# Mixing weights kept split across two passes, and the last norm's sums and spread set inside the first feed-forward blocks

## The chip, the cores and the metric

The program runs on one core of one Trainium2 chip. The metric is the device time of one launch in microseconds; a run is one execution, and the time given for a kernel is the median of its runs. TensorE (PE), VectorE (DVE), ScalarE (ACT), GpSimd (POOL) and SyncE (SP, which only issues transfers here) each execute their own instructions in order, and semaphores order them against each other.

## The reference

Two layers of a block on 1024 tokens and, in the first layer, 256 context tokens (1280 columns in layer 0, 1024 in layer 1), with 1024 features. All of it is computed in f32. What matters here is the end of each layer:

```
y = concatenate([retention, window attention, gated delta]) @ w_out[layer]
x = x + g1 * y
x = x + g2 * swiglu(rmsnorm(x, norm_ffn_w[layer]) * (1.0 + sc2) + sh2, w_ffn_in[layer], w_ffn_out[layer])
```

w_out is 1024 x 1024. swiglu is silu(h @ w1) * (h @ w3) @ w2 with 2816 inner features. The context tokens go through the same in layer 0 with their own scales. Everything ahead of the mixed outputs is left as it is by the change.

## The kernel before

Features lie on partitions (8 chunks of 128, index m for output and k for input), tokens along the free dimension. The tokens are cut into slices (`token_slices`): 256, 512 and 512 columns in layer 0, 512 and 512 in layer 1. The last slice is the "late" one, the others are "early". `mixed_ffn` (L1025) is one stage per layer: the mixing with w_out, the norm behind it, and the feed-forward loops.

A product of f32 precision takes three matmuls (`three_passes`, L927): the weight is split into a rounded part (hi) and the rest (lo), and so is the moving operand. A weight chunk of 128 x 1024 comes by one 512 KB transfer into `raw[u]`, ACT rounds it into `w_hi[u]` (`round`, L917), DVE subtracts and writes `w_lo[u]` (`rest`, L922); u alternates between two buffers, and one split is enough for one output chunk m.

The mixing has 16 passes (`passes`, L1061). Passes 0 to 7 take the early slices, m = 0 to 7, and passes 8 to 15 take the late slice, again m = 0 to 7. So each of the 8 weight chunks is loaded, rounded and split twice. In a pass PE does 8 k times 3 matmuls per slice into `bank[m % 2][slice]` (`pe_mix`, L1071); DVE then adds the product into x (`dve_add`, L1088, line L1095 in rows), ACT squares the new x (`square`, L359) and DVE adds the square to `total` (`gather`, L367). The list of each engine is written out by hand (`act_mix` L1098, `dve_mix` L1115): in pass i ACT squares and then rounds the weight of pass i+2, and DVE adds, gathers and then splits it.

The norm (`TurnedNorm`, L937) comes in two groups, early and late. Once `total` of a group is complete: PE sums over features (`pe_sums`, L965), ACT takes the root (L978), DVE inverts (L990) and lays it on diagonals (`dve_lay`, L995), PE spreads it over the partitions (`pe_spread`, L973). Then each slice takes 8 steps: DVE scales a chunk (L1006, into the two buffers of `ffn_prod`), ACT adds the shift and rounds (`act_round`, L985), DVE forms the rest (L1014). The results go into the tiles `ys` and `yr` (o_ys_hi, yr_lo and so on in rows), which held the mixer's outputs. The early group's sums and spread stand inside passes 8 and 9 (behind k = 4), and its steps are dealt out over passes 9 to 15 (`spots`, L1064), on DVE one of a pass's steps ahead of the gather and the weight split and the others behind them.

The feed-forward begins with `pe_first` (L1136), which does the first two output units u = 0 and 1. Before, it does u = 0 of the early slices, the late group's sums, u = 1 of the early slices, the late spread, and then both units of the late slice; each k of u = 0 waits for its norm step. Loops over the other units follow (`pe_up`, `pe_down`), in which `a_hi` and `a_lo` hold the gated products. These two tiles (128 x 5120 each) are idle until then. SP issues the weight transfers (L1263, L1267) as a buffer's split is done; POOL issues the eight loads of x (L1275) once the first two weight chunks have landed.

## Time and profile before

| | us |
|---|---|
| median of 3 runs | 3723.64 |
| lowest and highest run | 3721.9, 3729.55 |
| the profiled execution | 3734.98 |
| its span, first to last instruction | 3733.2 |
| PE busy | 3327.0 (89%) |
| DVE busy | 1644.3 (44%) |
| ACT busy | 1060.6 (28%) |
| mean granted TensorE clock | 0.931 |

The busy time of PE counts from a matmul's start to its modelled end, so successive matmuls overlap in it, and a matmul at the lower clock counts as longer busy. The distance from one start to the next tells more. Times of rows count from the start of the span. The stage `mixed_ffn` of layer 0 starts its matmuls at 977 us, that of layer 1 at 2884 us.

### The profile page before, as it was taken

What the parts mean: (1) busy time and instruction counts of PE and PEld (TensorE: products, weight loads), DVE (VectorE), ACT (ScalarE), POOL (GpSimd) and SP (SyncE); (2) the same over time, 40 slices, a digit from 0 to 9 for tenths busy, and PEclk for the clock granted to TensorE, in tenths of its full rate; (3) what the DMA queues carried; (4) which work ended last, traced back from release to release, by engine and by line L of the source; (5) the groups of instructions that cost most, each with busy time, mean ns of one, the idle gap of its engine ahead of it and who ended that gap; (6) DMA issues with size and microseconds to landing.
All of it is one profiled execution on the core that took longest, in us unless ns stands there. A gap on an engine that the chain in (4) does not pass through costs nothing. (4 is left out here: it accounts for less than half of the span.)

```text
span 3733.2 us, 56373 instructions
## 1 busy us (share of the span) xinstructions
PE 3327.0 (89%) x21762; PEld 2792.9 (75%) x21762; DVE 1644.3 (44%) x2735; ACT 1060.6 (28%) x1934; POOL 667.8 (18%) x762
## 2 busy tenths in 40 slices
PE   4989856977899999999999999757887999999998
PEld 2878745866778888888887788646775778888886
DVE  5365776632453322223136465775633532322234
ACT  3344134612232121121213244134512331122112
POOL 1232763222000000000001132762222000000000
PEclk7999967988999999999999999868997999999998
DMA  4456185086521111111112465285194311111111
GB/s 175 150 190 202 62 282 157 18 233 183 196 64 40 35 39 40 39 39 34 39 40 83 139 194 189 74 281 149 38 263 168 110 42 51 47 49 51 45 51 62
DMA packets 245240, 405.31 MB, mean 109 GB/s; under 512 B 76083, under 2 KB 146483, under 8 KB 244662
## 3 DMA queue, kind: packets, MB, share of 16 engines
q1 hardware_dynamic: 239222, 382.76, 32.9%
q0 software_dynamic: 5824, 19.93, 1.4%
q8 instruction: 126, 2.06, 0.2%
q14 instruction: 68, 0.56, 0.0%
HBM read 289.97 MB, written 100.56 MB: 105 GB/s over the span
## 5 line engine op out<-in xcount | busy, mean ns | idle before, releaser
L924 DVE TENSOR_TENSOR ffn_w_lo<-ffn_raw,ffn_w_hi 128x1024 fp32r<-128x1024 f32 x164 | 200.8, 1225 | 500.6 <-ACT ffn_w_hi L920 495.4
L849 PE MATMUL frt_acc<-frt_w_hi,frt_h_hi 128*128 128x472 f32 x928 | 364.7, 393 | 51.2 <-DVE frt_w_lo L728 26.5
L930 PE MATMUL ffn_bank<-yr_hi,ffn_w_hi 128*128 128x512 f32 (+1 forms) x1040 | 386.3, 371 | 24.9 <-DVE ffn_w_lo L924 22.0
L930 PE MATMUL ffn_bank<-o_ys_hi,ffn_w_hi 128*128 128x512 f32 (+1 forms) x1040 | 387.2, 372 | 7.1 <-DVE o_ys_lo L1014 6.1
L933 PE MATMUL ffn_bank<-o_ys_lo,ffn_w_hi 128*128 128x512 f32 (+1 forms) x1040 | 384.7, 370 | 0.0
L934 PE MATMUL ffn_bank<-o_ys_hi,ffn_w_lo 128*128 128x512 f32 (+1 forms) x1040 | 384.1, 369 | 0.0
L933 PE MATMUL ffn_bank<-yr_lo,ffn_w_hi 128*128 128x512 f32 (+1 forms) x1040 | 384.0, 369 | 0.0
L934 PE MATMUL ffn_bank<-yr_hi,ffn_w_lo 128*128 128x512 f32 (+1 forms) x1040 | 383.9, 369 | 0.0
L849 PE MATMUL frt_acc<-frt_w_hi,frt_h_lo 128*128 128x472 f32 x928 | 355.8, 383 | 0.0
L849 PE MATMUL frt_acc<-frt_w_lo,frt_h_hi 128*128 128x472 f32 x928 | 355.1, 383 | 0.0
L930 PE MATMUL ffn_bank<-ffn_a_hi,ffn_w_hi 128*128 128x512 f32 (+1 forms) x880 | 324.3, 368 | 0.8 <-DVE ffn_a_lo L1191 0.8
L933 PE MATMUL ffn_bank<-ffn_a_lo,ffn_w_hi 128*128 128x512 f32 (+1 forms) x880 | 324.3, 368 | 0.0
L934 PE MATMUL ffn_bank<-ffn_a_hi,ffn_w_lo 128*128 128x512 f32 (+1 forms) x880 | 323.7, 368 | 0.0
L920 ACT ACTIVATE ffn_w_hi<-ffn_raw 128x1024 fp32r<-128x1024 f32 x164 | 172.4, 1051 | 450.8 <-PE ffn_bank L930 443.1
L1234 DVE SCALAR_TENSOR_TENSOR x<-ffn_bank,mod,x 128x512 f32 (+3 forms) x240 | 166.7, 696 | 280.1 <-PE ffn_bank L934 279.3
L849 PEld LDWEIGHTS frt_acc<-frt_w_hi,frt_h_hi 128*128 128x128 f32 x928 | 179.0, 193 | 88.1 <-issue 26.4
L930 PEld LDWEIGHTS ffn_bank<-yr_hi,ffn_w_hi 128*128 128x128 f32 x1040 | 196.8, 189 | 64.1 <-DVE ffn_w_lo L924 25.3
L930 PEld LDWEIGHTS ffn_bank<-o_ys_hi,ffn_w_hi 128*128 128x128 f32 x1040 | 197.4, 190 | 45.2 <-issue 7.0
L1198 DVE TENSOR_TENSOR ffn_prod<-total,ffn_bank 128x512 f32<-128x512 f32 (+1 forms) x110 | 69.7, 634 | 360.9 <-PE ffn_bank L934 264.3
L934 PEld LDWEIGHTS ffn_bank<-o_ys_hi,ffn_w_lo 128*128 128x128 f32 x1040 | 197.0, 189 | 33.3
L933 PEld LDWEIGHTS ffn_bank<-o_ys_lo,ffn_w_hi 128*128 128x128 f32 x1040 | 197.6, 190 | 32.4 <-issue 0.5
L934 PEld LDWEIGHTS ffn_bank<-yr_hi,ffn_w_lo 128*128 128x128 f32 x1040 | 197.0, 189 | 32.9
(359 smaller groups left out, 5785.9 us busy)
## 6 DMA issues: line engine op xcount, KB each, us to landing
ffn_raw<-w_ffn SPq DMA_DIRECT2D x132, 512.0 KB, 3.6
x<-ada_w SPq DMA_DIRECT2D x15, 2048.0 KB, 9.2
proj<-frt_out SPq DMA_DIRECT2D x116, 236.0 KB, 2.0
x<-proj SPq DMA_DIRECT2D x60, 384.0 KB, 4.6
frt_raw<-w_in SPq DMA_DIRECT2D x96, 236.0 KB, 4.3
ffn_raw<-w_out SPq DMA_DIRECT2D x32, 512.0 KB, 3.7
met_pr<-proj SPq DMA_DIRECT2D x20, 768.0 KB, 6.5
met_vn<-pack SPq DMA_DIRECT2D x20, 640.0 KB, 6.3
```

The costliest lines, as they stand in the source:

```text
L849: mm = pe.matmul(acc[q % NA][:, 0:GW], a[:, k, tok], b[:, k, :], start=(k == 0 and i == 0), stop=(k == KC - 1 and i == 2))
L920: act.activation(self.hi[u][:], self.raw[u][:], ACT.Copy).then_inc(self.rounded[u], 1)
L924: dve.tensor_tensor(self.lo[u][:], self.raw[u][:], self.hi[u][:].bitcast(F32), ALU.subtract).then_inc(self.ready[u], 1)
L930: mm = pe.matmul(out, w_hi, b_hi, start=first, stop=False)
L933: pe.matmul(out, w_hi, b_lo, start=False, stop=False)
L934: return pe.matmul(out, w_lo, b_hi, start=False, stop=last)
L1198: dve.tensor_tensor(prod[:, t0:t0 + ln], sil[:, t0:t0 + ln], bank[1][s][:, 0:ln], ALU.mult).then_inc(free[1][s], 1)
L1234: dve.scalar_tensor_tensor(xs, bank[i][s][:, 0:ln], mod[:, bass.ds(m + 5 * KC, 1), v], xs, ALU.mult, ALU.add).then_inc(free[i][s], 1)
```

## The change

In both layers, after the change:

- There are nine weight splits instead of sixteen (`splits`: chunks 0 to 7, and chunk 5 once more). Chunks 0 to 4 are split into `a_hi` and `a_lo`, which have room for five, and stay there for both passes over the tokens. Chunks 5, 6, 7 and the second 5 use `w_hi` and `w_lo`.
- Passes 8 to 15 take m = 7, 6, 0, 1, 2, 3, 4, 5, so that the two chunks that are still in `w_hi` and `w_lo` come first.
- In passes 0 to 5 the split for two passes later stands ahead of the pass's squares (ACT) and ahead of its adds (DVE). The eighth split waits until PE has begun pass 6. The ninth stands in pass 10, the first feed-forward chunk's split in pass 12 and the second's behind pass 15.
- In passes 9 to 15 ACT takes the pass's first norm step ahead of the square, and DVE takes all steps of a pass ahead of the gather.
- The late group's sums stand inside `pe_first`, behind k = 4 of the last early slice of u = 0, and the late spread stands right behind that slice, ahead of u = 1 of the early slices.

```
...
-    def __init__(self, st, x, total, scratch, slices, name=""):
-        self.x, self.total, self.scratch, self.slices = x, total, scratch, slices
+    def __init__(self, st, x, total, scratch, slices, name="", order=range(KC)):
+        self.x, self.total, self.scratch, self.slices, self.order = x, total, scratch, slices, order
...
     def square(self, act, m, s):
...
         to = self.total[:, t0:t0 + n] if m == 0 else self.scratch[j % 2][:, 0:n]
-        act.activation(to, self.x[:, m, t0:t0 + n], ACT.Square).then_inc(self.squared, 1)
+        act.activation(to, self.x[:, self.order[m], t0:t0 + n], ACT.Square).then_inc(self.squared, 1)
...
         t0, n = self.slices[s]
...
         self.used = [st.sem(f"w_used{u}") for u in range(2)]
-    def round(self, act, u, n):
+    def round(self, act, u, n, first=False):
         act.wait_ge(self.landed[u], n * 16 + 16)
-        act.wait_ge(self.used[u], n + u)
+        if not first:
+            act.wait_ge(self.used[u], n + u)
...
     def rest(self, dve, u, n):
...
     early_s, late_s = list(range(NS - 1)), [NS - 1]
-    MU, MB = KC, KC // 2
+    MU, MB = 1, KC // 2
...
     h = [[ys[half][:, k] if k < 4 else yr[half][:, k - 4] for k in range(KC)] for half in range(2)]
...
-        sq_mix = [Squares(st, x, total, spare, [slices[s] for s in early_s], "early_"), Squares(st, x, total, spare, [slices[s] for s in late_s], "late_")]
+        second = [7, 6, 0, 1, 2, 3, 4, 5]
+        sq_mix = [Squares(st, x, total, spare, [slices[s] for s in early_s], "early_"), Squares(st, x, total, spare, [slices[s] for s in late_s], "late_", second)]
...
         full = [[st.sem(f"full{i}{s}") for s in range(NS)] for i in range(2)]
...
         weights_first = st.sem("weights_first")
-        passes = [(i, i % MU, i // MU) for i in range(2 * MU)]
+        kept = a_hi[:].rearrange("p j n -> p (j n)"), a_lo[:].rearrange("p j n -> p (j n)")
+        KEEP = 5
+        splits = [0, 1, 2, 3, 4, 5, 6, 7, 5]
+        m_landed = [st.sem(f"m_landed{r}") for r in range(2)]
+        m_rounded, m_ready, m_begun = st.sem("m_rounded"), st.sem("m_ready"), st.sem("m_begun")
+        stored = lambda n: [kept[i][:, n * DM:(n + 1) * DM] if n < KEEP else (w.hi, w.lo)[i][1 if n in (6, 8) else 0][:] for i in range(2)]
+        passes = [(i, m, 0) for i, m in enumerate(range(KC))] + [(KC + i, m, 1) for i, m in enumerate(second)]
+        split_of = list(range(KC)) + [7, 6, 0, 1, 2, 3, 4, 8]
         group = [early_s, late_s]
-        gathers = [(MU - 1) * len(g) for g in group]
+        gathers = [(KC - 1) * len(g) for g in group]
         spots = [2, 3, 3, 2, 2, 2, 2] if NS == 3 else [1, 1, 1, 1, 1, 1, 2]
-        def early_steps(m):
-            done = sum(spots[:max(m - 1, 0)])
-            return list(norm.steps(0))[done:done + (spots[m - 1] if m else 0)]
+        def early_steps(q):
+            done = sum(spots[:max(q - 1, 0)])
+            return list(norm.steps(0))[done:done + (spots[q - 1] if q else 0)]
         def pe_mix(pe, i, m, g):
-            n, u = divmod(i, 2)
-            pe.wait_ge(w.ready[u], n + 1)
+            q = i % KC
+            u = q % 2
+            n = split_of[i]
+            if n < 7:
+                pe.wait_ge(m_ready, n + 1)
+            else:
+                pe.wait_ge(w.ready[n - 7], 1)
+            hi, lo_w = stored(n)
...
                 t0, ln = slices[s]
-                if m >= 2:
-                    pe.wait_ge(free[u][s], m // 2)
+                if q >= 2:
+                    pe.wait_ge(free[u][s], q // 2)
...
                     f = slice(k * P, (k + 1) * P)
-                    mm = three_passes(pe, bank[u][s][:, 0:ln], w.hi[u][:, f], w.lo[u][:, f], mixed_in(0, k)[:, t0:t0 + ln], mixed_in(1, k)[:, t0:t0 + ln],
-                                      k == 0, k == KC - 1, w.used[1 - u] if s == group[g][0] and k == 0 else None)
-                    if g == 1 and k == 4 and m == 0:
+                    mm = three_passes(pe, bank[u][s][:, 0:ln], hi[:, f], lo_w[:, f], mixed_in(0, k)[:, t0:t0 + ln], mixed_in(1, k)[:, t0:t0 + ln],
+                                      k == 0, k == KC - 1, {KC: w.used[1], KC + 1: w.used[0]}.get(i) if s == group[g][0] and k == 0 else None)
+                    if s == group[g][0] and k == 0:
+                        mm.then_inc(m_begun, 1)
+                    if g == 1 and k == 4 and q == 0:
                         norm.pe_sums(pe, 0, sq_mix[0].gathered, gathers[0])
-                    if g == 1 and k == 4 and m == 1:
+                    if g == 1 and k == 4 and q == 1:
...
                 mm.then_inc(full[u][s], 1)
-        def dve_add(dve, m, g):
-            u = m % 2
+        def dve_add(dve, i, m, g):
+            q = i % KC
+            u = q % 2
...
                 v = 1 if t0 < CTX else 0
-                dve.wait_ge(full[u][s], m // 2 + 1)
+                dve.wait_ge(full[u][s], q // 2 + 1)
...
                                          ALU.mult, ALU.add).then_inc(free[u][s], 1)
+        def act_split(act, n):
+            if n < 7:
+                act.wait_ge(m_landed[n % 2], n // 2 * 16 + 16)
+                act.activation(stored(n)[0], w.raw[1 - n % 2][:], ACT.Copy).then_inc(m_rounded, 1)
+            elif n == 7:
+                act.wait_ge(m_begun, 7)
+                w.round(act, 0, 0, True)
+            else:
+                act.wait_ge(m_begun, KC + 3)
+                w.round(act, 1, 0, True)
+        def dve_split(dve, n):
+            if n < 7:
+                hi, lo_w = stored(n)
+                dve.wait_ge(m_rounded, n + 1)
+                dve.tensor_tensor(lo_w, w.raw[1 - n % 2][:], hi.bitcast(F32), ALU.subtract).then_inc(m_ready, 1)
+            else:
+                w.rest(dve, n - 7, 0)
+        def splits_beside(i):
+            if i < 6:
+                return [i + 2]
+            return {KC + 2: [8]}.get(i, [])
         def act_mix(act):
-            for u in range(2):
-                w.round(act, u, 0)
+            for n in range(2):
+                act_split(act, n)
             for i, m, g in passes:
+                q = i % KC
+                steps = early_steps(q) if g == 1 else []
+                if g == 0:
+                    for n in splits_beside(i):
+                        act_split(act, n)
+                for step in steps[:1]:
+                    norm.act_round(act, step)
                 for j, s in enumerate(group[g]):
-                    act.wait_ge(free[m % 2][s], m // 2 + 1)
-                    sq_mix[g].square(act, m, j)
-                w.round(act, i % 2, i // 2 + 1)
+                    act.wait_ge(free[q % 2][s], q // 2 + 1)
+                    sq_mix[g].square(act, q, j)
+                if g == 1 and q == 0:
+                    norm.act_root(act, 0)
+                for step in steps[1:]:
+                    norm.act_round(act, step)
                 if g == 1:
-                    if m == 0:
-                        norm.act_root(act, 0)
-                    for step in early_steps(m):
-                        norm.act_round(act, step)
+                    for n in splits_beside(i):
+                        act_split(act, n)
+                if i == KC + 4:
+                    w.round(act, 0, 1)
+            w.round(act, 1, 1)
...
         def dve_mix(dve):
-            for u in range(2):
-                w.rest(dve, u, 0)
+            for n in range(2):
+                dve_split(dve, n)
             for i, m, g in passes:
-                steps = early_steps(m) if g == 1 else []
-                dve_add(dve, m, g)
-                if steps:
-                    norm.dve_step(dve, 0, steps[0])
+                q = i % KC
+                steps = early_steps(q) if g == 1 else []
+                if g == 0:
+                    for n in splits_beside(i):
+                        dve_split(dve, n)
+                dve_add(dve, i, m, g)
+                for step in steps:
+                    norm.dve_step(dve, 0, step)
                 for j in range(len(group[g])):
-                    sq_mix[g].gather(dve, m, j)
-                w.rest(dve, i % 2, i // 2 + 1)
-                if g == 1 and m == 0:
+                    sq_mix[g].gather(dve, q, j)
+                if g == 1 and q == 0:
                     norm.dve_lay(dve, 0)
-                for step in steps[1:]:
-                    norm.dve_step(dve, 0, step)
+                if g == 1:
+                    for n in splits_beside(i):
+                        dve_split(dve, n)
+                if i == KC + 4:
+                    w.rest(dve, 0, 1)
+            w.rest(dve, 1, 1)
...
                 norm.dve_step(dve, 1, step)
...
         def pe_first(pe):
-            def unit(u, s):
+            def unit(u, s, summing=False):
...
                     pe.wait_ge(w.ready[u], MU + 1)
...
                                       h[0][k][:, t0:t0 + ln], h[1][k][:, t0:t0 + ln], k == 0, k == KC - 1, begun)
+                    if summing and k == 4:
+                        norm.pe_sums(pe, 1, sq_mix[1].gathered, gathers[1])
...
             for s in early_s:
-                unit(0, s)
-            norm.pe_sums(pe, 1, sq_mix[1].gathered, gathers[1])
+                unit(0, s, s == early_s[-1])
+            norm.pe_spread(pe, 1, free[1], MB)
...
                 unit(1, s)
-            norm.pe_spread(pe, 1, free[1], MB)
...
                 unit(1, s)
...
             def _(sp):
-                for i, m, g in passes:
-                    if i >= 2:
-                        sp.wait_ge(w.ready[i % 2], i // 2)
-                    sp.dma_start(w.raw[i % 2][:], w_out[m]).then_inc(w.landed[i % 2], 16)
+                for n, m in enumerate(splits):
+                    if n >= 2:
+                        sp.wait_ge(m_ready, n - 1)
+                    sp.dma_start(w.raw[1 - n % 2][:], w_out[m]).then_inc(w.landed[n - 7] if n >= 7 else m_landed[n % 2], 16)
...
                         sp.wait_ge(w.ready[u], n + MU)
...
                 for u in range(2):
-                    pool.wait_ge(w.landed[u], 16)
+                    pool.wait_ge(m_landed[u], 16)
...
```

TensorE around the late group's sums and spread, layer 0 (L934 or L935 is the third matmul of a k, ffn_sums the sums, `ffn_bank<-total,ones` the spread). Before:

```order
L930 MATMUL ffn_bank<-yr_hi,ffn_w_hi 128x512
L933 MATMUL ffn_bank<-yr_lo,ffn_w_hi 128x512
L934 MATMUL ffn_bank<-yr_hi,ffn_w_lo 128x512
L965 MATMUL ffn_sums<-ones,total 128x2 x4
L930 MATMUL ffn_bank<-o_ys_hi,ffn_w_hi 128x256
```

After:

```order
L935 MATMUL ffn_bank<-yr_hi,ffn_w_lo 128x512
L966 MATMUL ffn_sums<-ones,total 128x2 x4
L931 MATMUL ffn_bank<-yr_hi,ffn_w_hi 128x512
L934 MATMUL ffn_bank<-yr_lo,ffn_w_hi 128x512
L935 MATMUL ffn_bank<-yr_hi,ffn_w_lo 128x512
L931 MATMUL ffn_bank<-yr_hi,ffn_w_hi 128x512
L934 MATMUL ffn_bank<-yr_lo,ffn_w_hi 128x512
L935 MATMUL ffn_bank<-yr_hi,ffn_w_lo 128x512
L931 MATMUL ffn_bank<-yr_hi,ffn_w_hi 128x512
L934 MATMUL ffn_bank<-yr_lo,ffn_w_hi 128x512
L935 MATMUL ffn_bank<-yr_hi,ffn_w_lo 128x512
L974 MATMUL ffn_bank<-total,ones 128x512
```

The sums moved from behind the last early slice of u = 0 to three k ahead of its end, and the spread, which stood behind u = 1 of the early slices (48 matmuls later), now comes ahead of them.

VectorE in pass 13 of layer 0 (L1095 or L1113 the add, L1006 or L1007 a step's scale, L1014 or L1015 its rest, L367 the gather, L924 the weight split). Before:

```order
L1095 SCALAR_TENSOR_TENSOR x<-ffn_bank,mod,x 128x512
L1006 SCALAR_TENSOR_TENSOR ffn_prod<-x,affn,ffn_bank 128x512
L1014 SCALAR_TENSOR_TENSOR o_ys_lo<-ffn_prod,mod,o_ys_hi 128x512
L367 TENSOR_TENSOR total<-total,ffn_sq 128x512
L924 TENSOR_TENSOR ffn_w_lo<-ffn_raw,ffn_w_hi 128x1024
L1006 SCALAR_TENSOR_TENSOR ffn_prod<-x,affn,ffn_bank 128x512
L1014 SCALAR_TENSOR_TENSOR o_ys_lo<-ffn_prod,mod,o_ys_hi 128x512
```

After:

```order
L1113 SCALAR_TENSOR_TENSOR x<-ffn_bank,mod,x 128x512
L1007 SCALAR_TENSOR_TENSOR ffn_prod<-x,affn,ffn_bank 128x512
L1015 SCALAR_TENSOR_TENSOR o_ys_lo<-ffn_prod,mod,o_ys_hi 128x512
L1007 SCALAR_TENSOR_TENSOR ffn_prod<-x,affn,ffn_bank 128x512
L1015 SCALAR_TENSOR_TENSOR o_ys_lo<-ffn_prod,mod,o_ys_hi 128x512
L367 TENSOR_TENSOR total<-total,ffn_sq 128x512
```

The weight split is gone from this pass, and the gather stands behind both steps.

VectorE at the start of the stage, layer 0. Before:

```order
L924 TENSOR_TENSOR ffn_w_lo<-ffn_raw,ffn_w_hi 128x1024 x2
L1095 SCALAR_TENSOR_TENSOR x<-ffn_bank,mod,x 128x256
L1095 SCALAR_TENSOR_TENSOR x<-ffn_bank,mod,x 128x512
L924 TENSOR_TENSOR ffn_w_lo<-ffn_raw,ffn_w_hi 128x1024
L1095 SCALAR_TENSOR_TENSOR x<-ffn_bank,mod,x 128x256
```

After:

```order
L1131 TENSOR_TENSOR ffn_a_lo<-ffn_raw,ffn_a_hi 128x1024 x3
L1113 SCALAR_TENSOR_TENSOR x<-ffn_bank,mod,x 128x256
L1113 SCALAR_TENSOR_TENSOR x<-ffn_bank,mod,x 128x512
L1131 TENSOR_TENSOR ffn_a_lo<-ffn_raw,ffn_a_hi 128x1024
L1113 SCALAR_TENSOR_TENSOR x<-ffn_bank,mod,x 128x256
```

The third split now stands ahead of the first adds.

## Rows read from the trace of the kernel before

**Rows 1.** Timeline of PE, layer 0, passes 8 on: start us, us, engine, line, operands, idle before

```profile
1045.35 0.39 PE L930 MATMUL ffn_bank<-yr_hi,ffn_w_hi 128*128 128x512 f32 x1
...
1052.16 0.39 PE L930 MATMUL ffn_bank<-yr_hi,ffn_w_hi 128*128 128x512 f32 x1
...
1056.80 1.70 PE L973 MATMUL ffn_bank<-total,ones 128*128 128x256 f32 x4 [1.08 <-DVE total L995]
...
1060.41 0.39 PE L930 MATMUL ffn_bank<-yr_hi,ffn_w_hi 128*128 128x512 f32 x1
...
1085.56 0.50 PE L930 MATMUL ffn_bank<-yr_hi,ffn_w_hi 128*128 128x512 f32 x1 [1.72 <-DVE ffn_w_lo L924]
...
1099.03 0.39 PE L930 MATMUL ffn_bank<-o_ys_hi,ffn_w_hi 128*128 128x256 f32 x1 [0.99 <-DVE ffn_w_lo L924]
```

**Rows 2.** Timeline of PE, layer 0, first feed-forward units

```profile
1107.48 0.95 PE L965 MATMUL ffn_sums<-ones,total 128*128 128x2 f32 x8
...
1116.72 1.02 PE L973 MATMUL ffn_bank<-total,ones 128*128 128x512 f32 x2
1120.21 0.76 PE L930 MATMUL ffn_bank<-o_ys_hi,ffn_w_hi 128*128 128x512 f32 x1 [2.48 <-DVE o_ys_lo L1014]
...
1128.80 0.50 PE L930 MATMUL ffn_bank<-yr_hi,ffn_w_hi 128*128 128x512 f32 x1 [0.47 <-DVE yr_lo L1014]
...
1129.68 0.50 PE L930 MATMUL ffn_bank<-yr_hi,ffn_w_hi 128*128 128x512 f32 x1
...
1130.49 0.40 PE L930 MATMUL ffn_bank<-o_ys_hi,ffn_w_hi 128*128 128x512 f32 x1
...
1135.97 0.28 PE L930 MATMUL ffn_bank<-o_ys_hi,ffn_w_hi 128*128 128x256 f32 x1
```

**Rows 3.** Timeline of PE, layer 1, passes 8 on and first feed-forward units

```profile
2929.71 0.39 PE L930 MATMUL ffn_bank<-yr_hi,ffn_w_hi 128*128 128x512 f32 x1
...
2940.95 1.10 PE L973 MATMUL ffn_bank<-total,ones 128*128 128x512 f32 x2 [1.32 <-DVE total L995]
2941.48 0.79 PE L930 MATMUL ffn_bank<-o_ys_hi,ffn_w_hi 128*128 128x512 f32 x1
2942.11 0.39 PE L933 MATMUL ffn_bank<-o_ys_lo,ffn_w_hi 128*128 128x512 f32 x1
...
2978.20 0.40 PE L930 MATMUL ffn_bank<-o_ys_hi,ffn_w_hi 128*128 128x512 f32 x1
...
3005.64 0.39 PE L930 MATMUL ffn_bank<-o_ys_hi,ffn_w_hi 128*128 128x512 f32 x1
```

**Rows 4.** Timeline of DVE, layer 0, its list for pass 13

```profile
1087.40 0.74 DVE L1006 SCALAR_TENSOR_TENSOR ffn_prod<-x,affn,ffn_bank 128x512 f32<-128x512 f32 x1
1089.75 0.75 DVE L1014 SCALAR_TENSOR_TENSOR o_ys_lo<-ffn_prod,mod,o_ys_hi 128x512 fp32r<-128x512 f32 x1 [1.61 <-ACT o_ys_hi L985]
1090.42 0.69 DVE L367 TENSOR_TENSOR total<-total,ffn_sq 128x512 f32<-128x512 f32 x1
1091.02 1.22 DVE L924 TENSOR_TENSOR ffn_w_lo<-ffn_raw,ffn_w_hi 128x1024 fp32r<-128x1024 f32 x1
```

**Rows 5.** Timeline of ACT, layer 0, its list for pass 13

```profile
1088.06 1.04 ACT L920 ACTIVATE ffn_w_hi<-ffn_raw 128x1024 fp32r<-128x1024 f32 x1
```

**Rows 6.** Timeline of DVE, layer 0: the late norm laid, the first split for the loops

```profile
1109.01 0.69 DVE L995 SCALAR_TENSOR_TENSOR total<-mats,ffn_root 128x512 f32<-128x512 f32 x1
...
1132.49 1.22 DVE L924 TENSOR_TENSOR ffn_w_lo<-ffn_raw,ffn_w_hi 128x1024 fp32r<-128x1024 f32 x1 [2.86 <-ACT ffn_w_hi L920]
```

**Rows 7.** Stretches: us, busy (instructions) of each engine, granted clock, DMA share, GB/s

```profile
980.00:985.00 5.00, 5.00 (x29) 4.39 (x29) 0.67 (x2) 0.42 (x1) 1.07 (x3) 0.97 1.01 413
1120.00:1125.00 5.00, 4.58 (x11) 2.85 (x12) 4.86 (x8) 2.17 (x3) 0.00 (x0) 0.66 0.00 0
```

**Rows 8.** Line L1263, the loads of w_out: issue to landing, us

```profile
DMA to landing us min/median/max: 3.3/3.7/8.2
```

**Rows 9.** Weight loads of TensorE by tile: duration ns min, median, max

```profile
L930 PEld LDWEIGHTS ffn_bank<-yr_hi,ffn_w_hi x1040: 186/188/330, 977.2 to 3684.8; 128*128 128x128 f32 x174
```

## Prediction

> **What bounds the kernel now.** I began with the page's busy table: TensorE (PE) is busy 89% of the span, and in the feed-forward loops it never stops, so time can only be won where PE waits. I then took PE's waits in the stretch from pass 8 of `mixed_ffn` to the end of `pe_first`, in both layers, and read that stretch in the timeline row by row. I measure from one start of a matmul to another, since busy time counts a slow or late matmul as work.
>
> The unit of measure is 24 matmuls of 512 columns (8 k, three each) without a wait: 1130.49 to 1135.97 is 5.48 us, 0.685 us for a k [rows 2].
>
> In layer 0 passes 8 to 15 run from 1045.35 to 1099.03, 53.68 us for eight such units, one set of sums and one spread [rows 1]. The reader is to see the bracket at 1085.56: PE stood until DVE had written `ffn_w_lo`. That split is late because DVE's list of a pass is longer than PE's pass. It holds the add (as long as a rest, 0.67), two scales and two rests (4 times 0.67), the gather (0.60), the split (1.22) and an idle 1.61 until ACT delivers `o_ys_hi`: together 6.8 us against 5.48 [rows 4]. The idle time comes from ACT's own list, in which the square and the 1.04 us of weight rounding stand ahead of the step's rounding [rows 5]. In layer 1 only one step falls to a pass, and passes 8 to 15 take 48.49 us, 2929.71 to 2978.20 [rows 3], nearly without these waits.
>
> Behind it, in layer 0, the spread stands at 1116.72 and the late slice's u = 0 begins only at 1120.21, then follows DVE's steps: k = 6 begins at 1128.80, 12.08 us after the spread, k = 7 at 1129.68, 12.96 after it, and the next unit at 1130.49, 13.77 after it [rows 2]. So the steps, which cannot begin before the spread, end this stretch, and PE's 5.48 us of work are spread over 13.77 less the spread. PE's loss there is more than the brackets of idle time tell, because it also ran slow: the granted clock of 1120 to 1125 is 0.66, a mix of 2.4 and 1.2 GHz after the idle 2.48 us [rows 2, 7].
>
> **The change: the splits.** Seven of sixteen splits go in each layer: 7 times 1.04 us of ACT and 7 times 1.22 of DVE, with seven transfers of 512 KB. On the path lies only what made PE late. The list of a pass such as pass 13 becomes 0.67 + 4 x 0.67 + 0.60 = 3.95 us, and the idle 1.61 goes too, since no rounding of weights stands there and the pass's first step is rounded ahead of the square. Passes 10 and 12 keep a split: 3.95 + 1.22 = 5.17, still under 5.48 (in layer 0 the steps of pass 10 are three of 256 columns, which come to no more). So PE becomes the one that ends each of passes 10 to 15. The weights of passes 8 to 14 were split long before.
>
> Pass 9 holds the early spread. It began 4.64 us into the pass where five k take 3.43, so 1.21 were lost to the lay [rows 1]. With 1.04 of rounding gone from ahead of the root and 1.22 of split from ahead of the lay, it comes in time. What is left of pass 9 beyond its unit is 8.25 - 5.48 - 1.21 = 1.56 for a spread of two slices, and of pass 8 it is 6.81 - 5.48 = 1.33 for the sums.
>
> Layer 0: 8 x 5.48 + 1.33 + 1.56 = 46.73 instead of 53.68, **6.95 us less**. Layer 1: sums of 8 matmuls cost 0.79 (1107.48 to 1116.72 is 9.24, and the same two slices without them, 1099.03 to 1107.48, are 8.45) [rows 1, 2]; a spread of one slice costs 0.53 until the next matmul and 0.40 more in that one (0.63 against 0.23), 0.93 [rows 3]. So 43.84 + 0.79 + 0.93 = 45.56 instead of 48.49, **2.93 less**.
>
> **The change: sums and spread of the late norm.** From the start of the sums to the lay's end are 2.22 us (1107.48 to 1109.01 + 0.69) [rows 2, 6]. In the new place the sums and three k lie between, 0.79 + 2.06 = 2.85, so PE does not wait for the lay, by 0.6 us. The sums themselves need the last gather. In layer 0 they stand a 256 slice and five k behind pass 15, over 6 us, and DVE is done by 4. In layer 1 they stand 3.43 us behind it, and DVE needs the add, one scale, two rests and the gather, 3.3 us, and some tenths for signals and the last rounding: I count a **wait of 0.6**.
>
> After the spread DVE and ACT have 13.77 us of work to give the late slice's last k, as now. In layer 0 PE now has ahead of the end of that unit: spread 0.93, u = 1 of the early slices 8.45, the unit itself 5.48: 14.86, more than 13.77 (and k = 6 would begin at 13.49, against 12.08). No wait is left. Layer 0 from 1099.03: 8.45 + 9.24 + 0.93 + 5.48 = 24.10, against 31.46 to 1130.49, **7.36 less**. In layer 1 the early part is one slice: 0.93 + 5.48 + 5.48 = 11.89 is shorter than 13.77, so the last k still wait, 1.88 us together. 5.48 + 0.79 + 0.60 + 13.77 = 20.64 against 27.44 (2978.20 to 3005.64) [rows 3], **6.80 less**.
>
> What is late next: the loop's first split ended 3.22 us after u = 1 of the late slice began, and PE wanted it at 5.48 [rows 2, 6]; this chain starts from the same unit as before, so the 2.3 us of room stay. The loops behind are PE's alone.
>
> **The change: splits ahead of adds in the first eight passes.** In passes 0 to 5 DVE's adds are now queued behind the split for two passes on, and that behind a landing. PE in pass 2 waits for the add of pass 0. The longest landing of a w_out chunk is 8.2 us, against a median of 3.7 [rows 8]. From PE's start: 8.2 + 1.04 + 1.22 + 0.67 = 11.1 us, and pass 2 begins at 2 x 5.48 = 11.0 in layer 1 and at 2 x 8.45 = 16.9 in layer 0. So even the longest costs a tenth: zero. The load behind pass 2 has left the worst behind it. The wait of the eighth split for pass 6's start holds ACT and DVE, but adds of pass 5 are wanted only by pass 7, 8.45 or 5.48 us later.
>
> The long landing is seen beside the loads of x, when the DMA engines were busy 1.01 of the time at 413 GB/s [rows 7]. The Trainium skill (DMA: Bandwidth & Descriptors, "Issuing engines are not separate DMA queues") says that transfers issued by SP and by POOL share the same 16 engines and interleave. It speaks against putting adds behind these landings; the trace agrees (8.2 against 3.3), and by this rule the cost is what the worst landing above gives.
>
> **Sum.** 6.95 + 7.36 + 2.93 + 6.80 = 24.0 us. The profiled execution of 3734.98 becomes 3711.0. It lies 11.3 above the median of the runs shown, and I take the same distance again: 3723.64 - 24.0 = **3699.6**. Ends of the unknowns: the waits in layer 1 may be gone too (2.5 us more), and restarts after small gaps may stay (some 2 us less); the runs before spread over 3721.9 to 3729.55. Alone this case spans 3695 to 3704.
>
> **Rivals.**
> - *Clock.* After the change layer 1 still has thin work at its last three k. Before, the clock fell there after an idle stretch and thin work. If it falls again, now next to full units of PE, the stretch is not hidden: 5.8 us at half clock do 2.9 us less. 3702.5, chance 0.07. The Trainium skill (TensorE: Matmul & The Clock Gate, Part 1) says that the gate halves the clock when the array has been idle and gives it back after sustained work. The trace agrees with the first [rows 7]. By that rule the clock should hold in layer 0, where no idle time is left.
> - *DVE or ACT still ends passes 9 to 15* (an ordering wait takes the place of the split). For it: the first step's rounding now stands ahead of the square, and all steps ahead of the gather, so each add's square comes later. Against: 1.5 us of room in most passes. It costs the 9.9 of both layers: 3709.5, chance 0.08.
> - *The late spread waits for the lay*, the room being 0.6 us, and PE idles in the middle of its blocks. At the most all 14.2 of these blocks are lost: 3713.8, chance 0.05.
> - *The adds behind landings.* Were a landing twice the longest seen, pass 2 would come 8.3 us late in layer 1 and 2.4 in layer 0: 3710.3, chance 0.04.
> - *Slower: weights read from the kept tiles.* Passes 0 to 4 and 10 to 14 load their weights from tiles of 20 KB a partition, which ACT and DVE write at the same time: 360 weight loads in layer 0 and 240 in layer 1. A load takes 188 ns, at most 330 [rows 9], against 228 from matmul to matmul. If the kept ones held PE up by 40 ns each, 24 us were gone, and from there it is slower; at 53 ns the time is 3731.4. Against: the same tiles serve as moving operands in the loops without a gap. Chance 0.03.
> - *It changes nothing*, because PE's lateness comes from elsewhere: 3723.6, chance 0.02.
>
> **How the numbers follow.** The forecast has 0.71. The range 3693 to 3711 takes in the forecast with the spread of runs, the clock, the DVE and the landing case and leaves out the other three. A measurement of this kernel can tell about 0.2%, 7.4 us, from no change; all but the last two cases are faster by more: faster 0.94, same 0.03, slower 0.03.
>
> **What would show it.** Right: in layer 0 pass 8 to `pe_first` in 46 to 47 us, with no bracket naming `ffn_w_lo`; the late u = 0 of layer 0 without a bracket and the granted clock at 1.00; in layer 1 short brackets at its last three or four k; the spread of layer 1 behind its place by under 1 us. Wrong: brackets at passes 2 to 4 that name the add, a distance above 0.23 us between the matmuls of passes 10 to 14, or loops that are longer than now.

## The result, and the profile after

| | before | after |
|---|---|---|
| median of the runs taken side by side, us | 3723.09 (4 runs, 3721.9 to 3729.55) | 3692.14 (4 runs, 3691.62 to 3692.91) |
| ratio, with its interval | | 0.9915 [0.9899, 0.993] |
| the profiled execution, us | 3734.98 | 3691.62 |
| mean granted TensorE clock | 0.931 | 0.934 |

The kernel is faster by 31.0 us between medians where 24.0 were forecast, and 3692.14 lies 0.9 us below the range of 3693 to 3711. The direction is as forecast; the question is where the other 7 us come from.

The head of the page after, span and busy times:

```profile
span 3689.8 us, 56303 instructions
PE 3305.6 (90%) x21762; PEld 2785.7 (75%) x21762; DVE 1619.4 (44%) x2721; ACT 1049.2 (28%) x1920; POOL 673.8 (18%) x762
```

DVE is busy 25 us less and ACT 11. The 14 splits of 1.22 us that are gone come to 17 of it on DVE, and the 14 roundings of 1.04 to 15 on ACT, more than its whole difference. The timeline of PE after, layer 0 (start us, us, engine, line, operands, and in brackets the idle time before it), the places of [rows 1, 2]:

```profile
1029.62 0.39 PE L931 MATMUL ffn_bank<-yr_hi,ffn_w_hi 128*128 128x512 f32 x1
...
1036.43 0.39 PE L931 MATMUL ffn_bank<-yr_hi,ffn_w_hi 128*128 128x512 f32 x1
...
1039.84 1.45 PE L974 MATMUL ffn_bank<-total,ones 128*128 128x256 f32 x4
...
1043.21 0.39 PE L931 MATMUL ffn_bank<-yr_hi,ffn_a_hi 128*128 128x512 f32 x1
...
1075.86 0.28 PE L931 MATMUL ffn_bank<-o_ys_hi,ffn_w_hi 128*128 128x256 f32 x1
...
1082.16 0.95 PE L966 MATMUL ffn_sums<-ones,total 128*128 128x2 f32 x8
...
1085.12 1.02 PE L974 MATMUL ffn_bank<-total,ones 128*128 128x512 f32 x2
...
1094.32 0.39 PE L931 MATMUL ffn_bank<-o_ys_hi,ffn_w_hi 128*128 128x512 f32 x1
...
1099.76 0.39 PE L931 MATMUL ffn_bank<-o_ys_hi,ffn_w_hi 128*128 128x512 f32 x1
...
1105.20 0.28 PE L931 MATMUL ffn_bank<-o_ys_hi,ffn_w_hi 128*128 128x256 f32 x1
```

No bracket is left. Passes 8 to 15 run from 1029.62 to 1075.86, 46.24 us against 53.68; the sums stand inside the second early slice at 1082.16, the spread behind it, and the late slice's two units are 5.44 us each (1094.32, 1099.76, 1105.20).

The same timeline in layer 1, against [rows 3]:

```profile
2896.20 0.39 PE L931 MATMUL ffn_bank<-yr_hi,ffn_w_hi 128*128 128x512 f32 x1
...
2941.55 0.39 PE L931 MATMUL ffn_bank<-o_ys_hi,ffn_w_hi 128*128 128x512 f32 x1
...
2945.43 1.05 PE L966 MATMUL ffn_sums<-ones,total 128*128 128x2 f32 x8 [0.32 <-DVE total L367]
...
2948.49 1.02 PE L974 MATMUL ffn_bank<-total,ones 128*128 128x512 f32 x2
...
2959.13 0.50 PE L931 MATMUL ffn_bank<-yr_hi,ffn_w_hi 128*128 128x512 f32 x1 [0.48 <-DVE yr_lo L1015]
...
2960.58 0.51 PE L931 MATMUL ffn_bank<-yr_hi,ffn_w_hi 128*128 128x512 f32 x1 [0.48 <-DVE yr_lo L1015]
...
2962.26 0.39 PE L931 MATMUL ffn_bank<-o_ys_hi,ffn_w_hi 128*128 128x512 f32 x1
```

Here brackets remain only in the two places where the forecast kept a wait: 0.32 for the last gather, and two of 0.48 at k = 5 and 6 of the late unit. The stretches behind them, as in [rows 7] (us, busy time and instructions of PE, PEld, DVE, ACT and POOL, granted clock, DMA share, GB/s), the first two in layer 0, the third in layer 1:

```profile
1085.00:1090.00 5.00, 5.00 (x33) 4.28 (x32) 3.61 (x6) 2.09 (x3) 0.00 (x0) 1.00 0.01 3
1095.00:1100.00 5.00, 5.00 (x24) 4.14 (x23) 2.87 (x5) 3.65 (x6) 0.00 (x0) 1.00 0.00 0
2955.00:2960.00 5.00, 4.52 (x19) 2.88 (x17) 4.89 (x8) 2.27 (x4) 0.00 (x0) 1.00 0.00 0
```

The granted clock is 1.00, 2.4 GHz, in all three, also in the thin stretch of layer 1. Before it was 0.66 in the stretch at 1120.

**Where the time went, stage by stage.** From the first TensorE matmul of one stage to that of the next, worked out from the traces. `ffn` is `mixed_ffn` with its norm and loops, and in layer 0 also the norm at the start of the next front; a stage `front` is counted from its first product (L849 before). The last row counts everything else between the first matmul of the program and the first of its final norm, also stages that have no row here (both windows, the second front and gate, the modulation at the start).

```
us            before   b_same  e_sums  e_keep  e_order    after  a_again
front         415.26   418.25  416.75  416.88   418.17   411.78   415.45
meet, L0      113.39   111.30  108.63  109.53   112.96   108.31   110.16
scan, L0      142.86   137.32  141.25  140.74   136.93   137.44   136.38
gate, L0       70.96    69.88   71.51   71.76    70.61    70.89    70.62
ffn, L0      1055.29  1055.91 1048.85 1048.72  1040.08  1040.04  1040.01
meet, L1      110.99   108.82  108.92  113.12   106.92   108.55   106.64
scan, L1      126.05   121.78  124.71  119.38   122.29   124.46   121.11
ffn, L1       828.09   828.07  824.00  822.58   818.94   818.79   819.01
both ffn     1883.39  1883.98 1872.85 1871.30  1859.03  1858.83  1859.03
all but ffn  1813.27  1800.56 1808.92 1807.39  1800.79  1794.06  1795.83
```

The two `ffn` stages gained 24.6 us (15.25 and 9.30). Of the 43.4 us between the two profiled executions the other 18.8 lie outside them, where the code is the same in both kernels. That is what the experiments had to settle: does the change reach into them, or do they vary by themselves?

### The profile page after: what moved, and what is told of

Its sections match the earlier page's. It is cut to its first block and busy times, and to the rows that moved or that the text cites. A ratio compares the mean times of both kernels' runs of the same rounds, so it can differ in the third digit from the quotient of the medians.

```text
span 3689.8 us, 56303 instructions
## 1 busy us (share of the span) xinstructions
PE 3305.6 (90%) x21762; PEld 2785.7 (75%) x21762; DVE 1619.4 (44%) x2721; ACT 1049.2 (28%) x1920; POOL 673.8 (18%) x762
## 5 line engine op out<-in xcount | busy, mean ns | idle before, releaser
L849 PE MATMUL frt_acc<-frt_w_hi,frt_h_hi 128*128 128x472 f32 x928 | 365.5, 394 | 47.2 <-DVE frt_w_lo L728 21.9
L925 DVE TENSOR_TENSOR ffn_w_lo<-ffn_raw,ffn_w_hi 128x1024 fp32r<-128x1024 f32 x136 | 166.7, 1225 | 482.7 <-ACT ffn_w_hi L921 477.6
L849 PE MATMUL frt_acc<-frt_w_hi,frt_h_lo 128*128 128x472 f32 x928 | 356.2, 384 | 0.0
L849 PE MATMUL frt_acc<-frt_w_lo,frt_h_hi 128*128 128x472 f32 x928 | 356.2, 384 | 0.0
L931 PE MATMUL ffn_bank<-o_ys_hi,ffn_w_hi 128*128 128x512 f32 (+1 forms) x940 | 348.2, 370 | 0.0
L931 PE MATMUL ffn_bank<-yr_hi,ffn_w_hi 128*128 128x512 f32 (+1 forms) x940 | 346.8, 369 | 1.0 <-DVE yr_lo L1015 1.0
L934 PE MATMUL ffn_bank<-o_ys_lo,ffn_w_hi 128*128 128x512 f32 (+1 forms) x940 | 346.7, 369 | 0.0
L935 PE MATMUL ffn_bank<-yr_hi,ffn_w_lo 128*128 128x512 f32 (+1 forms) x940 | 346.2, 368 | 0.0
L935 PE MATMUL ffn_bank<-o_ys_hi,ffn_w_lo 128*128 128x512 f32 (+1 forms) x940 | 346.2, 368 | 0.0
L934 PE MATMUL ffn_bank<-yr_lo,ffn_w_hi 128*128 128x512 f32 (+1 forms) x940 | 346.1, 368 | 0.0
L934 PE MATMUL ffn_bank<-ffn_a_lo,ffn_w_hi 128*128 128x512 f32 (+1 forms) x880 | 324.6, 369 | 0.0
L935 PE MATMUL ffn_bank<-ffn_a_hi,ffn_w_lo 128*128 128x512 f32 (+1 forms) x880 | 324.0, 368 | 0.0
L921 ACT ACTIVATE ffn_w_hi<-ffn_raw 128x1024 fp32r<-128x1024 f32 x136 | 143.0, 1052 | 450.8 <-PE ffn_bank L931 438.9
L849 PEld LDWEIGHTS frt_acc<-frt_w_hi,frt_h_hi 128*128 128x128 f32 x928 | 179.6, 194 | 83.1 <-issue 24.2
L931 PEld LDWEIGHTS ffn_bank<-o_ys_hi,ffn_w_hi 128*128 128x128 f32 x940 | 177.3, 189 | 30.7 <-issue 1.0
L934 PEld LDWEIGHTS ffn_bank<-o_ys_lo,ffn_w_hi 128*128 128x128 f32 x940 | 177.4, 189 | 30.1 <-issue 1.0
L935 PEld LDWEIGHTS ffn_bank<-o_ys_hi,ffn_w_lo 128*128 128x128 f32 x940 | 177.1, 188 | 29.6
L935 PEld LDWEIGHTS ffn_bank<-yr_hi,ffn_w_lo 128*128 128x128 f32 x940 | 177.3, 189 | 29.3
```

Of the source, the lines that this page charges most:

```text
L849: mm = pe.matmul(acc[q % NA][:, 0:GW], a[:, k, tok], b[:, k, :], start=(k == 0 and i == 0), stop=(k == KC - 1 and i == 2))
L921: act.activation(self.hi[u][:], self.raw[u][:], ACT.Copy).then_inc(self.rounded[u], 1)
L925: dve.tensor_tensor(self.lo[u][:], self.raw[u][:], self.hi[u][:].bitcast(F32), ALU.subtract).then_inc(self.ready[u], 1)
L931: mm = pe.matmul(out, w_hi, b_hi, start=first, stop=False)
L934: pe.matmul(out, w_hi, b_lo, start=False, stop=False)
L935: return pe.matmul(out, w_lo, b_hi, start=False, stop=last)
```

## The experiments

The theory: the change is worth 24 to 25 us, all in the two `ffn` stages, by the two parts of the forecast, and the rest is the spread of the other stages from one execution to the next. The rivals: the change makes other stages faster too; or the parts are worth something else than the trace said.

**The kernel before, once more.** No edit; it measures the spread.

> The kernel before once more, unchanged, timed and profiled. In the first comparison the two mixing and feed-forward stages gave 15.2 and 9.3 us (24.5, against 24.0 forecast), and 18.9 us of the profiled 43.4, or some 6.5 of the 31.0 us between the medians, lay in stages that the change does not touch (front, meet and scan of both layers). Theory A, chance in those stages: their transfers land at different times in each execution, and this second profile has span and stage times that differ from the first by several us, with nothing changed; its medians stay near 3723. Theory B, the change itself makes them faster (less traffic, a shorter program): this profile repeats the first within 2 us in each stage.

Measured: 3721.92 us (10 runs, 3710.7 to 3726.57), ratio 1.0002 [0.9989, 1.0016]. The kernel before, run beside it 25 times, spread over 3704.24 to 3730.72. In the table its `ffn` stages are the profiled kernel's within 0.6 us, while its other stages are 12.7 us shorter, with the same instructions. One place of it, PE's waits in the scan of layer 0 (line waited for; total us, times, longest), first of the kernel before:

```profile
PE scn_b_k L1958 <- DMA early_rkv<-pack: 9.4, 3, 3.7
```

and of this run:

```profile
PE scn_b_k L1958 <- DMA early_rkv<-pack: 6.8, 2, 4.3
```

2.6 of that stage's 5.5 us are shorter waits for this transfer. So the profiled execution that the forecast started from was a long one, in stages that the change doesn't touch. The rival's expectation, each stage repeated within 2 us, did not come true.

**Only the sums and the spread moved.**

```diff
-            def unit(u, s):
+            def unit(u, s, summing=False):
...
+                    if summing and k == 4:
+                        norm.pe_sums(pe, 1, sq_mix[1].gathered, gathers[1])
...
             for s in early_s:
-                unit(0, s)
-            norm.pe_sums(pe, 1, sq_mix[1].gathered, gathers[1])
+                unit(0, s, s == early_s[-1])
+            norm.pe_spread(pe, 1, free[1], MB)
             for s in early_s:
                 unit(1, s)
-            norm.pe_spread(pe, 1, free[1], MB)
```

> Only the late norm's sums and spread are moved into the first feed-forward blocks; all sixteen splits stay as before. By the forecast's steps this is worth 7.4 us in layer 0 and, since the last gather of layer 1 is later here (the sums wait about 1.1 us for it), some 6.3 in layer 1: 13.7 us, 3709.4. Passes 9 to 15 still show PE waiting for ffn_w_lo (about 5 us in layer 0). If the excess of 6.5 us in other stages belongs to this part, the median is near 3703; if the two parts only work together, it stays above 3716.

Measured: 3714.53 us (10 runs, 3702.87 to 3720.06), ratio 0.9978 [0.9961, 0.9995], above the 3709.4 that was expected; the `ffn` stages take 10.5 us less than before and 11.1 less than in b_same. Layer 0 keeps its slow passes (53.65) and gains its 7.5 in the first blocks (18.56 + 5.44 + 5.44, against 21.18 + 10.28 + 5.48). Layer 1 gains 4.1, where some 6.3 were expected. PE's timeline of layer 1 shows why:

```profile
2972.44 1.05 PE L965 MATMUL ffn_sums<-ones,total 128*128 128x2 f32 x8 [1.11 <-DVE total L367]
...
2973.99 0.63 PE L934 MATMUL ffn_bank<-yr_hi,ffn_w_lo 128*128 128x512 f32 x1
2974.42 0.63 PE L930 MATMUL ffn_bank<-yr_hi,ffn_w_hi 128*128 128x512 f32 x1
...
2987.72 0.50 PE L930 MATMUL ffn_bank<-yr_hi,ffn_w_hi 128*128 128x512 f32 x1 [0.48 <-DVE yr_lo L1014]
...
2989.17 0.50 PE L930 MATMUL ffn_bank<-yr_hi,ffn_w_hi 128*128 128x512 f32 x1 [0.48 <-DVE yr_lo L1014]
```

The sums wait 1.11 us for the last gather, against 0.32 with the splits gone: in this kernel a rounding and a split still stand in the last passes' lists. That wait was in the expectation. What was not is the clock behind it: the matmuls between sums and spread start 0.43 us apart (2973.99, 2974.42), where the kernel after has 0.23, and the granted clock of the two stretches is 0.88 and 0.78, a mix of 2.4 and 1.2 GHz:

```profile
2970.00:2975.00 5.00, 3.89 (x19) 2.98 (x19) 3.93 (x6) 1.89 (x4) 0.00 (x0) 0.88 0.25 62
2975.00:2980.00 5.00, 5.00 (x17) 3.67 (x16) 1.74 (x4) 1.07 (x2) 0.00 (x0) 0.78 0.24 93
```

From the end of the sums to the spread this kernel takes 3.62 us (2973.36 to 2976.98) and the kernel after 2.15 (2946.34 to 2948.49). So 1.5 us of the missing 2.2 went with the clock. It is what the forecast's clock rival feared, and it came where a longer wait was left; in the kernel after, whose wait is 0.32, it did not.

**Only the kept weights and the new order of passes.** The kernel after with the first blocks of before, that is the diff above turned round.

> Only the mixing weights are kept (with their new order of passes and lists); sums and spread of the late norm stand where they stood before. Measured so far with both parts, passes 8 to 15 gave 7.4 us in layer 0 and 3.1 in layer 1: 10.6 us, 3712.5, with no wait for ffn_w_lo, and the gap of about 2.5 us with a lower granted clock behind the late spread back in both layers. If the excess of 6.5 us belongs to the kept weights (seven loads less in each layer, a shorter program), the median is near 3706.

Measured: 3712.94 us (10 runs, 3702.82 to 3717.36), ratio 0.9979 [0.9961, 0.9997]; the `ffn` stages take 12.1 to 12.7 us less, where 10.6 were expected. Neither part has the excess of the whole kernel: with it the medians were expected near 3703 (e_sums) and 3706 (e_keep), and they are 3714.53 and 3712.94. Passes 8 to 15 fall to 46.23 in layer 0 and 45.35 in layer 1, as in the kernel after. The late unit stays at 10.26, and PE's waits from pass 8 to the end of the first blocks in layer 0 name no split any more:

```profile
PE ffn_bank L931 <- DVE o_ys_lo L1015: 2.7, 2, 2.5
PE ffn_bank L931 <- DVE yr_lo L1015: 1.4, 3, 0.5
```

where the same view of b_same has

```profile
PE ffn_bank L930 <- DVE ffn_w_lo L924: 4.6, 4, 1.7
PE ffn_bank L930 <- DVE o_ys_lo L1014: 2.9, 2, 2.5
PE ffn_bank L930 <- DVE yr_lo L1014: 1.4, 3, 0.5
PE ffn_bank L973 <- DVE total L995: 1.1, 1, 1.1
```

Each part removes its own brackets and leaves the other's. The granted clock falls at the late unit here too, in layer 1:

```profile
2975.00:2980.00 5.00, 2.53 (x7) 1.66 (x6) 4.67 (x7) 2.42 (x4) 0.00 (x0) 0.73 0.00 0
```

One thing was not in the expectation: the early blocks of layer 1 take 15.30 instead of 17.17 us, since the last pass's rest is no longer behind a split. Before, PE waited for it inside u = 0:

```profile
2984.69 0.51 PE L930 MATMUL ffn_bank<-yr_hi,ffn_w_hi 128*128 128x512 f32 x1 [1.44 <-DVE yr_lo L1014]
```

The forecast had these 1.9 us in its sum, but under the sums and the spread; they belong to the splits.

The parts give 10.8 and 12.4 us (means over both comparisons), 23.2 together, against 24.8 for both at once. Most of the difference is not an interaction of the two. The norm at the start of the next front, which the `ffn` row of layer 0 takes in, took 11.2 and 11.1 us in these two profiles, 10.0 in before and b_same and 9.9 in after, with the same code. Counted from the start of pass 8 to the end of `pe_first` in both layers, the stretch that the change touches takes 172.0 us before, 160.1 in e_sums, 159.4 in e_keep and 147.1 after: the parts give 11.9 and 12.6, together 24.5, and both at once 24.9. The 0.4 us that are left stand in layer 1, where e_sums has the slower clock.

**The order of the lists put back.** The kernel after, but in passes 9 to 15 with the place that square, steps and gather had before.

```diff
-                for step in steps[:1]:
-                    norm.act_round(act, step)
                 for j, s in enumerate(group[g]):
...
-                for step in steps[1:]:
+                for step in steps:
                     norm.act_round(act, step)
...
-                for step in steps:
+                for step in steps[:1]:
                     norm.dve_step(dve, 0, step)
...
+                for step in steps[1:]:
+                    norm.dve_step(dve, 0, step)
```

> The changed kernel, but in passes 9 to 15 ACT squares first and then rounds, and DVE takes one step ahead of the gather and the others behind it, as before. With no split in these passes DVE's list is 3.95 us and an idle 0.6 while ACT squares and rounds, 4.5 us against PE's 5.48: by my theory PE still ends every pass and the time is that of the changed kernel within 2 us, 3692 (the sums of layer 1 wait less, by 0.3). The rival, that DVE and ACT need the new order of their lists, expects waits in passes 10 to 15 and 3 to 9 us more, 3695 to 3701.

Measured: 3695.56 us (4 runs, 3690.28 to 3698.37), ratio 0.9925 [0.9896, 0.9954]. By the median alone this is outside the expected 3692 within 2 and inside the rival's 3695 to 3701, but single runs of the unchanged kernel after reach from 3687.7 to 3696.4 (below). The stages decide: the `ffn` stages take 1859.03 against 1858.83, and passes 10 to 15 5.44 us each, as in the kernel after. DVE's timeline, here its list for pass 10, shows the idle time back in its list, and that it costs nothing:

```profile
1059.54 0.75 DVE L1113 SCALAR_TENSOR_TENSOR x<-ffn_bank,mod,x 128x512 f32<-128x512 f32 x1 [1.71 <-PE ffn_bank L935]
...
1061.39 0.49 DVE L1015 SCALAR_TENSOR_TENSOR o_ys_lo<-ffn_prod,mod,o_ys_hi 128x256 fp32r<-128x256 f32 x1 [0.71 <-ACT o_ys_hi L986]
```

DVE stands 0.71 us for the rounding, but its add ahead of it had waited 1.71 for PE: the list has room for both. Of the idle 1.61 us that the forecast took off a pass [rows 4] some 0.7 is still here, 0.66 in the lists of passes 12 to 15; the weight rounding made the other 0.9 to 1.0, and the new order takes the rest away. PE gains nothing from that rest.

**The kernel after, once more.** No edit.

> The changed kernel once more. The two changed stages gave 24.6 us in both profiles that hold both parts. If the other 6.4 us of the first comparison were chance in the stages ahead (their sum was 1794 to 1813 us in six profiles of the same code), more runs spread over 10 us or more and their median lies 24 to 26 below that of the runs before on the same chip, near 3695. If the change brings them, this stays at 3692 with its four runs' spread of 1.3 us, and the profile shows the other stages at 1794 us again.

Measured: 3693.33 us (6 runs, 3687.74 to 3696.41), the kernel before beside it 3722.54, ratio 0.9927 [0.9907, 0.9947]. Its `ffn` stages are those of the profile after within 0.2 us, and its other stages 1.8 us longer. The runs spread over 8.7 us, nearly the 10 expected of chance, but the median is 29.2 below the runs beside it, not 24 to 26, and the other stages nearly repeat the 1794 us that the rival named. This run alone does not decide between the two.

**The mixing and feed-forward stages alone, before and after.** Left out are front, meet, window, scan and gate of both layers, so the output is another; the stages get copies of x as their inputs, and modulations of 0.5.

> The two changed stages by themselves, as before the change: front, meet, window, scan and gate of both layers are left out, the mixing takes copies of x as its input, and the modulations are constants. If the runs' spread comes from the stages left out, these runs agree within 3 us, where the whole kernel spreads over 26. By the stage times of the profiles it takes 1884 us and some 70 for the loads and modulation at the start, 1950 to 1970.

> The same with the changed stages (front, meet, window, scan and gate left out, inputs as in only_before). Against only_before I expect 24.5 us less, within 1.5: the gain of the change without the noise of the other stages. The rival, that the change also helps the stages around it by its lighter traffic, has nothing to help here and so predicts the same 24.5 here and more in the whole kernel.

Measured: 2023.26 us (2021.86 to 2024.65) and 2000.18 (1999.01 to 2000.85), **23.1 us** less, at the low end of the 24.5 within 1.5 that was expected. The runs of each lie within 2.8 us of one another, against 26 for the 68 of the whole kernel; with four runs of each that is weak by itself, as the first four of the kernel after lay within 1.3 us. Passes 8 to 15 of layer 0 go from 53.80 to 47.15 and the first blocks from 37.12 to 29.69, much as in the whole kernel. The times as such missed their 1950 to 1970: the two stages take 1922.8 and 1898.9 us here, with the filling of layer 1's inputs in them, and a unit without a wait takes 5.56 us, not 5.44, at a granted clock of 1.00; why is open. With the other stages gone the change is worth 23 us and most of the spread is gone too.

**An earlier start.** PE waits 8.53 us for the first weights of the stage in the kernel after (its PE timeline):

```profile
961.51 0.58 PE L931 MATMUL ffn_bank<-yr_hi,ffn_a_hi 128*128 128x256 f32 x1 [8.53 <-DVE ffn_a_lo L1131]
```

So the first chunk was loaded, rounded and split in two halves, and PE waits for the second only ahead of k = 4:

```diff
+            if n == 0:
+                for e in range(2):
+                    c = slice(e * DM // 2, (e + 1) * DM // 2)
+                    act.wait_ge(m_landed[2] if e == 0 else m_landed[0], 16)
+                    act.activation(stored(n)[0][:, c], w.raw[1][:, c], ACT.Copy).then_inc(m_rounded, 1)
...
+                    if i == 0 and s == group[g][0] and k == KC // 2:
+                        pe.wait_ge(m_ready, 2)
```

> The changed kernel with one more edit: the first weight chunk of each mixing stage is loaded, rounded and split in two halves, and TensorE starts on the first half. Its wait at the start of the stage was 8.5 us, of which rounding and splitting of the whole chunk are 1.04 and 1.22. Halves bring the start forward by about 1.1 us in each layer, 2 us in all, if nothing else is late; too little for the median, so the stage times decide. If the landing sets the start and the second half comes late, the stages are equal.

Measured: 3695.98 us (5 runs, 3682.17 to 3701.08), ratio 0.9939 [0.9917, 0.9961]: not better than the kernel after. The wait did become shorter:

```profile
955.96 0.58 PE L931 MATMUL ffn_bank<-yr_hi,ffn_a_hi 128*128 128x256 f32 x1 [6.79 <-DVE ffn_a_lo L1140]
```

but passes 0 to 7 took 69.23 us instead of 68.12, so 1.1 of the 1.7 us were lost again. The stretches from that start show it, the granted clock being the third number from the end:

```profile
955.00:960.00 5.00, 4.04 (x19) 4.04 (x20) 2.61 (x3) 1.87 (x3) 2.41 (x5) 0.50 0.52 192
960.00:965.00 5.00, 5.00 (x23) 4.38 (x23) 1.71 (x2) 1.47 (x2) 1.95 (x4) 0.85 1.00 377
```

PE had idled before this start, and the clock was 0.50, 1.2 GHz, until 5.54 us after the first matmul; in the kernel after it was back 2.94 us after it. PE started earlier and ran longer at half clock. In layer 1 it was 4.80 against 5.45, the other way, and there passes 0 to 7 took 45.91 against 46.22. The profile of this run lasted 3682.17 us, the lowest of all, with an `ffn` sum of 1859.22 like the others: its other stages took 1784.4. That sum cannot show an earlier start, since it counts from the stage's first matmul; the gain would stand in the row ahead. There the gate of layer 0 took 67.51 us against 70.89 in after and that of layer 1 59.86 against 60.67; the wait itself is 1.7 us shorter in layer 0 and 1.6 in layer 1 (8.44 became 6.81). So the trace shows a shorter wait, partly given back in layer 0, and the median shows no gain.

**An empty addition.** Seven tiny instructions on ACT and seven on DVE at the start of each mixing stage, in both kernels. They change the program and give PE nothing to do.

```diff
+                for r in range(7):
+                    act.activation(warms[:, r:r + 1], eps[:], ACT.Sqrt)
...
+                for r in range(7):
+                    dve.memset(idle[:, r:r + 1], 0.0)
```

> The kernel before with seven instructions of 128x1 elements added on ACT and on DVE at the start of each mixing stage, where both engines wait 4 to 8 us for the first weight chunk. They cost nothing on the path, so the sum of the two changed stages stays at 1883.4 to 1884.0. The medians of kernels so far lie up to 4.5 us from what their stage times say (changed kernel 4.5 lower, e_sums and e_keep some 3.5 higher, against 3721.8 of 51 runs of the kernel before). Theory: such offsets come with any change of a program, so this median moves by 2 to 5 us from the runs before beside it, either way. Rival: nothing moves without a reason, and the median is that of the kernel before within 1.5 us.

> The changed kernel with the same fourteen idle instructions on ACT and DVE, which gives it the number of instructions that the kernel before has there. The two changed stages stay at 1859.0. If the 4.5 us beyond the stages' gain belong to the shorter program, the median rises from 3692.7 to about 3697; if they belong to the lighter traffic of the change, it stays within 1.5 us of 3692.7; if they are an offset of the one program, it lands anywhere from 3690 to 3701.

Measured: on the kernel before 3725.06 us (12 runs, 3715.55 to 3728.93), beside 3718.37 of it without them (17 runs), ratio 1.0012 [1.0002, 1.0022]; on the kernel after 3694.4 (6 runs, 3689.61 to 3706.43), ratio to the kernel before 0.9936 [0.9922, 0.995]. Against the expectations: the median of b_pad lies 6.7 us above that of the runs beside it and 4.5 by the ratio, but 3.8 above that of all 68 runs, so it speaks for an offset as far as the runs beside it can be trusted. Its `ffn` sum is 1885.6, not 1883.4 to 1884.0. Two places make that up, with code as in b_same. In layer 1 u = 1 of the early slice took 10.68 us instead of 9.05, with a granted clock of 0.86 in a stretch of it where b_same has 1.00:

```profile
2979.50:2984.50 5.00, 5.00 (x20) 3.97 (x20) 0.00 (x0) 0.00 (x0) 0.00 (x0) 0.86 0.00 0
```

The norm at the start of the next front took 11.2 instead of 10.0, behind a longer wait; passes 0 to 7 gave 1.1 back. The median of a_pad lies 1.7 above the 3692.7 it was compared with, between the readings, and decides nothing. The profiled execution of a_pad is 14.8 us longer than that of after, and all of it (14.75) lies outside the `ffn` stages (1808.81 against 1794.06; `ffn` 1858.96 against 1858.83).

**All runs together.** The profiled execution is 38.3 to 38.7 us plus the two sums of the table in every profile of the whole kernel taken here. The `ffn` sum holds within 2.2 us for the kernels with before's `ffn` stages (before, b_same and b_pad, 1883.4 to 1885.6) and within 0.4 for those with both parts (1858.8 to 1859.2). The other stages take 1784 to 1813 us in the ten profiles: 1800.6 to 1813.3 in the five without both parts, 1784.4 to 1808.8 in the five with both. From the start of pass 8 to the end of `pe_first`, both layers together, before and b_same take 172.0 and 171.9 us, and the five with both parts 147.0 to 147.1: so much the change is worth where it stands, 24.9 us, and it repeats within 0.1 (b_pad, with its slower clock in one block, takes 173.5). The kernel before ran 68 times in all: median 3721.3, mean 3720.1, standard deviation 5.9, 3704.2 to 3730.7. The four kernels with both parts (after, e_order, a_pad, e_start; 25 runs) have a mean of 3694.2, 25.8 below it. The kernel after alone, in 10 runs, has 3692.3, 27.7 below, and the other three, in 15 runs, 3695.5, 24.6 below. With one part alone it is the other way: e_sums lies 7.1 below and e_keep 9.0, in 10 runs each, where their stages give 10.8 and 12.4.

## Why the prediction was right or wrong

**Direction and mechanism: right**, with the terms measured so:

| term, us less | forecast | measured | alone |
|---|---|---|---|
| layer 0, passes 8 to 15 | 6.95 | 7.44 | 7.44 in e_keep |
| layer 0, first blocks | 7.36 | 7.57 | 7.5 in e_sums |
| layer 1, passes 8 to 15 | 2.93 | 3.14 | 3.14 in e_keep |
| layer 1, first blocks | 6.80 | 6.73 | 4.4 in e_sums, 1.9 in e_keep |
| both stages, from start to end | 24.0 | 24.6 | 10.8 + 12.4 |

- *The unit.* A unit without a wait is 5.44 us, not 5.48; eight of them explain 0.3 of the 0.5 us in layer 0. The other 0.2 is the early spread, 1.34 us in pass 9 and not 1.56.
- *The waits of layer 1.* For the sums 0.6 was forecast and 0.32 came; for the last k 1.88 us in all were forecast, and the unit takes 7.41 against 5.44, 1.97. The working by DVE's steps behind the spread held. No wait is left in layer 0, as forecast. What the forecast gave to each part did not hold: it had 9.9 us for the splits and 14.2 for sums and spread, and alone they gave 12.4 and 10.8. In layer 1 1.9 us of the first blocks go with the splits, and without the splits' part a slower clock takes 1.5.
- *The order of the lists* was credited with part of the idle 1.61, and rightly: 0.66 to 0.71 of it is back in e_order. But PE ends the passes either way, so on the path the order is worth nothing.
- *Splits ahead of adds.* The longest landing of a w_out chunk rose from 8.2 to 9.0 us, as the loads' row after shows:

```profile
DMA to landing us min/median/max: 3.3/4.5/9.0
```

  DVE's list of the first passes is late by it, but the add of pass 0 comes long before PE needs its bank again:

```profile
968.48 1.23 DVE L1131 TENSOR_TENSOR ffn_a_lo<-ffn_raw,ffn_a_hi 128x1024 fp32r<-128x1024 f32 x1 [5.78 <-ACT ffn_a_hi L1119]
969.62 0.48 DVE L1113 SCALAR_TENSOR_TENSOR x<-ffn_bank,mod,x 128x256 f32<-128x256 f32 x1
```

  Passes 0 to 7 of layer 0 take 68.12 us against 68.17; in layer 1 they take 46.22 against 45.67. The difference stands in pass 0 alone (8.14 against 7.59), where the full clock comes back at different times (5.45 us after its start, against 4.29); passes 1 to 7 take 8.34 us each in layer 0 and 5.44 in layer 1, in all ten profiles. Zero was right.
- *Weights from kept tiles.* The loads from `ffn_a_hi` are as long as those of [rows 9]. The 28 of all 600 kept ones that took over 200 ns lie in the first 3 us of the stage in layer 0 and the first 5.4 us in layer 1, at the half clock; passes 10 to 14 run at 5.44 us. So the slower rival falls:

```profile
L931 PEld LDWEIGHTS ffn_bank<-yr_hi,ffn_a_hi x100: 187/188/332, 961.5 to 2935.2; 128*128 128x128 f32 x100
```

- *Clock, and DVE or ACT still ending passes.* The clock is 1.00 in the three stretches shown, and passes 8 to 15 show no bracket. Both rivals fall for this kernel; e_sums shows the clock rival where the wait is 1.11 us. What stood at DVE now waits for PE, as its list for pass 14 in layer 0 shows:

```profile
1070.69 0.75 DVE L1113 SCALAR_TENSOR_TENSOR x<-ffn_bank,mod,x 128x512 f32<-128x512 f32 x1 [1.32 <-PE ffn_bank L935]
```

- *What is late next.* The loop's first split ends 3.0 us after u = 1 of the late slice began, PE wants it at 5.44. The room is there.

**The step that failed** is the end of "Sum", the rest of the program. It was put at the same distance as before ("I take the same distance again"), and "the runs before spread over 3721.9 to 3729.55" was taken as what it can do. The case alone got 3695 to 3704, some 4.5 us to each side with the terms' own 2 to 2.5 in them, and the whole range ended 6.6 us below the forecast. Three runs that happened to agree were read as the spread. The same kernel spans 26.5 us over 68 runs, and the three lay on the upper side of them (median 3723.64 against 3721.3). A forecast of 3720 to 3721 less 24.6 is 3695 to 3696, and with a standard deviation of 5.9 for a single run that of a median of four is 3, of the difference of two such medians 4, so by this estimate (twice that 4) the range has to reach some 8 us to each side, down to about 3688. 3692.14 is then an ordinary result of the 24.6 us that the stages show. Of the 7.5 us from the forecast of 3699.6 down to 3692.14 the terms make 0.6, the base 3.6 (3723.64 against the mean of 3720.1), and 3.3 are left.

**What stays open** is the last 3 us: ten runs of the kernel after lie 27.7 us below the mean of before, the stages say 24.6 and the pair without the other stages 23.1. Chance draws of the waiting stages would do, and so would a small offset of each particular program. For the second speaks that e_sums and e_keep gain 3.6 and 3.4 us less than their stages say and that the padded kernel before, whose addition should cost nothing, came out at 1.0012 [1.0002, 1.0022]; for the first that the intervals of e_sums and e_keep take in what their stages say, and that the three other kernels with both parts lie 24.6 below before. That the two parts together also make the other stages faster is the third reading; over all 25 runs with both parts it has 1.2 us to explain (25.8 against 24.6), about the standard error of that difference. No run here tells the three apart, and none is shown.

## What to carry to other kernels

Sum the terms by stage from one matmul start to another, and ask of the stages that the change does not touch how much they vary: where they wait for landings, three runs that agree say little about it, and the range must hold their spread as well as that of the terms. An engine whose list is longer than the pass sets the pass. Here it was enough to take out of the list what was computed a second time; the new order inside it brought nothing more. Cost each part with the other present and absent: in layer 1 the first blocks gained 4.4 and 1.9 us by the parts alone and 6.7 by both, since the wait of 1.11 us that one part leaves was followed by a lower clock and the wait of 0.32 was not.

## What was not expected of the hardware

- Stages with unchanged instructions differ by up to 29 us (1784.4 to 1813.3) between executions. PE's waits for landings are part of it, as shown in the scan. In the meet of layer 0 they moved the other way: 1.1 us in one wait before, 6.7 in four after, while the stage as a whole got 5.1 us shorter; its waits for DVE's `met_hp` went from 53.1 to 47.8 us, and why is open. The waits of before and of after, in this order:

```profile
PE met_b_y L1509 <- DMA met_vn<-pack: 1.1, 1, 1.1
```

```profile
PE met_b_y L1571 <- DMA met_vn<-pack: 6.7, 4, 2.7
```

  Without these stages four runs spread over 2.8 us in 2023, and four over 1.8 in 2000.
- Behind a wait of 1 to 1.5 us the clock fell in some executions and held in others. Behind the same wait of 1.44 us for `yr_lo` in layer 1 the granted clock stayed at 1.00 in before and b_same and fell to 0.80 and 0.86 in two stretches of b_pad, which cost 1.6 us; behind 1.11 us it fell in e_sums. A cost taken from one trace can miss this.
- The stretch at half clock behind an idle start is not tied to when PE starts: the full clock came back 2.94, 3.00, 3.61, 4.72 and 5.54 us after the first matmul of layer 0 in after, a_again, b_pad, b_same and e_start, and 2.9 to 3.1 us after it in the other five profiles. In e_start a start that was 1.7 us earlier gave 1.1 of it back; b_same shows a late return without an earlier start, so that the one brought the other is not shown. The Trainium skill (TensorE: Matmul & The Clock Gate, Part 1) says that the moment of the return depends on where the first matmul lands in a count that a start of work does not reset, and gives half a microsecond to each side for it. The traces agree with the first, in that the return does not keep a fixed distance from the start; the five times lie 2.6 us apart, more than half a microsecond to each side.
